# All 32 experts of the first pass in one loop, with an expert of no tokens at each end, and TensorE's three counts in registers

## The reference

```python
logits = h @ w_router + b_router                  # h (320, 1024), 32 experts
top_val, top_idx = lax.top_k(logits, 4)
gates = softmax(top_val)
for e in range(32):                               # what the blocks of rows amount to
    xb = h[tokens of e]
    x_glu, x_lin = jnp.split(xb @ w_gu[e] + b_gu[e], 2, axis=-1)        # 1024 -> 2048
    x_glu, x_lin = jnp.minimum(x_glu, 7.0), jnp.clip(x_lin, -7.0, 7.0)
    act = x_glu * sigmoid(1.702 * x_glu) * (x_lin + 1.0)
    out = (act @ w_down[e] + b_down[e]) * gate                          # 1024 -> 1024
    acc[tokens of e] += out
x = x + gate2 * acc
```

## Time and profile before

| | us |
|---|---|
| median of 3 runs | 1277.75 (1271.48 to 1280.69) |
| the profiled execution | 1283.42 |
| its span in the profile | 1281.6 |
| PE busy | 1108.4 (86%) |
| DVE, ACT, POOL busy | 416.6, 194.3, 44.0 |

### The profile page before, as it was taken

One profiled execution on the slowest core, in us unless ns is written; L12 is line 12 of the kernel. 1 busy time (PEld: TensorE's weight loads), 2 busy tenths in 40 slices (PEclk: granted clock), 3 DMA queues, 4 the chain that ended last, 5 costly groups with the idle time before them and its releaser, 6 DMA issues.

```text
span 1281.6 us, 21966 instructions
## 1 busy us (share of the span) xinstructions
PE 1108.4 (86%) x7288; PEld 463.7 (36%) x7289; DVE 416.6 (33%) x1295; ACT 194.3 (15%) x427; POOL 44.0 (3%) x27
## 2 busy tenths in 40 slices
PE   4999998976858888679979998999999979869986
PEld 0667664643223223223323332333333323223332
DVE  2133635434215222223233224233223323322233
ACT  2323242122101000011101111011111101101100
POOL 0141110002000000000000000000000000000000
PEclk8998997986979989999999999999999999988988
DMA  9963218730979999999999999999999999999992
GB/s 379 344 232 119 91 68 326 280 131 26 395 313 423 422 422 422 422 422 422 421 422 422 421 423 422 421 422 422 422 422 421 422 422 422 422 422 422 421 421 104
DMA packets 76889, 454.99 MB, mean 355 GB/s; under 512 B 9868, under 2 KB 14732, under 8 KB 24524
## 3 DMA queue, kind: packets, MB, share of 16 engines
q1 hardware_dynamic: 70304, 449.76, 85.6%
q10 hardware_dynamic: 6540, 4.60, 1.3%
HBM read 451.17 MB, written 3.17 MB: 355 GB/s over the span
## 4 chain that ended last, share of the span: by engine, by line
PE 58%; DMA 26%; issue 5%; SPq 5%; DVE 4%; ACT 2%; DVEq 0%; POOL 0%; ACTq 0%
DMA ring<-w_gu 20%; PE psum L907 12%; PE psum L941 11%; PE psum L593 6%; PE psum L900 4%; SPq L507 4%; DMA ring<-w_down 4%; PE psum L978 3%; PE psum L862 3%; PE psum L802 3%; PE psum L897 2%; PE psum L602 2%; DMA ring<-w_ada 2%; PE psum L557 2%; PE psum L870 1%
## 5 line engine op out<-in xcount | busy, mean ns | idle before, releaser
L907 PE MATMUL psum<-ring,work 128*32 128x512 f32 (+1 forms) x1792 | 328.8, 632 | 46.2 <-DMA ring<-w_gu 39.1
L941 PE MATMUL psum<-ring,work 128*32 128x256 f32 (+1 forms) x1760 | 205.8, 470 | 22.5 <-issue 11.2
L1699 DVE SCALAR_TENSOR_TENSOR x<-psum,tiny,x 128x256 f32<-128x256 f32 (+1 forms) x512 | 155.2, 376 | 203.0 <-PE psum L978 203.0
L907 PEld LDWEIGHTS psum<-ring,work 128*32 128x32 f32 (+1 forms) x1792 | 84.1, 126 | 247.1 <-issue 141.1
L1668 DVE TENSOR_SCALAR work<-csb 96x128 bf16<-96x128 f32 x64 | 15.4, 280 | 406.3 <-PE psum L907 337.5
L1050 ACT ACTIVATE work<-psum 128x256 f32<-128x256 f32 (+5 forms) x215 | 88.2, 430 | 336.8 <-PE psum L941 210.7
L941 PEld LDWEIGHTS psum<-ring,work 128*32 128x32 f32 (+1 forms) x1760 | 78.3, 123 | 134.6 <-issue 100.1
L1305 ACT ACTIVATE work<-work 128x128 f32<-128x128 f32 (+2 forms) x64 | 24.2, 378 | 574.3 <-DVE work L1683 574.3
L593 PE MATMUL psum<-h,ring 128*128 128x320 f32 x320 | 91.9, 445 | 1.2 <-ACT h L1085 1.2
L978 PE MATMUL psum<-work 32*128 32x320 f32 (+1 forms) x576 | 79.6, 478 | 4.7 <-issue 3.3
L593 PEld LDWEIGHTS psum<-h,ring 128*128 128x128 f32 x320 | 62.3, 196 | 27.4 <-issue 3.7
(11 more groups left out here) (213 smaller groups left out, 704.8 us busy)
## 6 DMA issues: line engine op xcount, KB each, us to landing
ring<-w_gu SPq DMA_DIRECT2D x256, 1024.0 KB, 25.7
ring<-w_down SPq DMA_DIRECT2D x128, 1024.0 KB, 23.4
ring<-w_ada SPq DMA_DIRECT2D x12, 2048.0 KB, 9.0
ring<-w_in SPq DMA_DIRECT2D x7, 2048.0 KB, 30.4
ring<-w_out SPq DMA_DIRECT2D x2, 2048.0 KB, 11.1
x<-xT SPq DMA_DIRECT2D x1, 1280.0 KB, 6.0
yT<-x SPq DMA_DIRECT2D x2, 640.0 KB, 4.1
work<-b_exp ACTq DMA_DIRECT2D x3, 384.0 KB, 16.5
```

Of the source, the lines that this page charges most:

```text
L907: last = mm(o, xg[:, kk, 0:m], cols(ring[:, kk, :]), start=False, stop=kk == KD - 1)
L941: last = mm(o, actT[:, kk, cols], ring[:, GU_UNITS + kk // 2, c1_:c1_ + n], start=False, stop=kk == 7)
L1699: last = stt(x[:, f, cols], bank[SPREAD_BANKS[u]][:, cols], mod[:, 40 + f, sq_:sq_ + 1], x[:, f, cols], ALU.mult, ALU.add)
```

## The change

`passes` runs the first pass as one loop over all 32 experts. What an expert does for its neighbours now happens at both ends too. Ahead of expert 0 stands an expert of no tokens: its output `otok` and its scatter matrix `spread` are zeros that POOL writes, so expert 0's body scatters zeros and DVE adds them to `x`; the semaphores `otok_ready`, `spread_ready` and `acc_ready` start 1, 1 and 8 higher, and the thresholds move with them. Behind expert 31 stands another: `cnti` has a zero ahead of and two behind the 32 counts, `rank` and the constant `stack` have a 33rd column, so expert 31's body gathers and turns an empty selection. PE loads three counts with one instruction (`reg_load`) into registers, once ahead of the loop and then in each expert behind units 0 to 2, for the next expert. Passes 1 and 2 keep their form.

```diff
         def passes(eng, start, expert, finish):
             eng.wait_ge(cnt_ready, 1)
             start(0, 0, 0)
-            expert(0, 0, 0, True, False)
             most = eng.value_load(cmaxi[0:1, 0:1], min_val=0, max_val=T)
-            with eng.Fori(1, NE - 1) as e:
+            with eng.Fori(0, NE) as e:
                 expert(e, e, 0, False, False)
-            expert(NE - 1, NE - 1, 0, False, True)
             finish(NE - 1, 0)
...
             def start(turn, e, b):
+                at = ahead(turn, b)
                 n = count(pe, e)
...
+                by_rows(pe, n, b, lambda groups: (gather(at, groups), turn_x(at, groups)))
+                if isinstance(b, int):
+                    pe.reg_load(counts, cnti[0:1, 0:3])
...
             def expert(turn, e, b, begins, ends):
-                n = count(pe, e)
-                before = None if begins else count(pe, e - 1)
-                after = None if ends else count(pe, e + 1)
-                pe.wait_ge(xg_ready, turn + 1)
-                by_size(pe, n, b, lambda groups: (up_bias(turn, groups), gate_up(0, 3, turn, groups)))
+                if begins:
+                    before, n, after = None, count(pe, e), count(pe, e + 1)
+                else:
+                    before, n, after = [pe.snap(r) for r in counts]
+                at = ahead(turn, b)
+                pe.wait_ge(xg_ready, at + 1)
+                by_size(pe, n, b, lambda groups: (up_bias(at, groups), gate_up(0, 3, turn, groups)))
+                if not ends:
+                    pe.reg_load(counts, cnti[0:1, bass.ds(e + 1, 3)])
                 if not begins:
                     spread_out(0, turn - 1, before, b)
...
             def add(i, turn):
-                if i == 0 and not (isinstance(turn, int) and turn == 0):
-                    v.wait_ge(acc_ready, turn * 8)
+                if i == 0:
+                    v.wait_ge(acc_ready, turn * 8 + 16)
...
-            cp(cnti, bank[5][:, 96:128])
+            nc.vector.memset(rank[:, :, NE:NE + 1], -1.0)
+            nc.vector.memset(cnti[:, 0:1], 0)
+            nc.vector.memset(cnti[:, NE + 1:NE + 3], 0).then_inc(acc_ready, 8)
+            cp(cnti[:, 1:NE + 1], bank[5][:, 96:128])
...
+            g.wait_ge(state_stored, 16 * 2)
+            g.wait_ge(logit_ps, 1)
+            nc.gpsimd.memset(otok[:, 0:256], 0.0).then_inc(otok_ready, 1)
+            nc.gpsimd.memset(spread, 0.0).then_inc(spread_ready, 1)
```

More of the change, by code:

```diff
@@ L440, in count, with ahead @@
         def count(eng, e):
-            return eng.value_load(cnti[0:1, bass.ds(e, 1)], min_val=0, max_val=T)
+            return eng.value_load(cnti[0:1, bass.ds(e + 1, 1)], min_val=0, max_val=T)
+        def ahead(turn, b):
+            return turn if isinstance(b, int) else turn + 1
         def by_size(eng, n, b, body):
@@ L834, in _ @@
             for tt, (t0, n) in enumerate(TILES):
-                last = mm(bank[7][0:n, tt * NE:(tt + 1) * NE], lgT[:, t0:t0 + n], K("stack"), start=True, stop=True)
+                last = mm(bank[7][0:n, tt * NE:(tt + 1) * NE], lgT[:, t0:t0 + n], K("stack")[:, 0:NE], start=True, stop=True)
             last.then_inc(logit_ps, 1)
@@ L989, in scatter @@
                         part(u, FEATURES[4 * i + u], 4, 512, spread_b, False, True).then_inc(sc_ps, 1)
+            counts = [pe.alloc_register(f"count{i}") for i in range(3)]
             def start(turn, e, b):
+                at = ahead(turn, b)
                 n = count(pe, e)
-                pe.wait_ge(pick_ready, turn * 3 + 3)
+                pe.wait_ge(pick_ready, at * 3 + 3)
                 if not isinstance(b, int):
-                    pe.wait_ge(acc_ready, turn * 8)
-                by_rows(pe, n, b, lambda groups: (gather(turn, groups), turn_x(turn, groups)))
+                    pe.wait_ge(acc_ready, turn * 8 + 16)
+                by_rows(pe, n, b, lambda groups: (gather(at, groups), turn_x(at, groups)))
+                if isinstance(b, int):
+                    pe.reg_load(counts, cnti[0:1, 0:3])
             def spread_out(i, turn, n, b):
                 if i == 0:
-                    pe.wait_ge(otok_ready, turn + 1)
-                    pe.wait_ge(spread_ready, turn + 1)
+                    pe.wait_ge(otok_ready, turn + 2)
+                    pe.wait_ge(spread_ready, turn + 2)
                 by_size(pe, n, b, lambda groups: scatter(i, turn, groups))
             def expert(turn, e, b, begins, ends):
-                n = count(pe, e)
-                before = None if begins else count(pe, e - 1)
-                after = None if ends else count(pe, e + 1)
-                pe.wait_ge(xg_ready, turn + 1)
-                by_size(pe, n, b, lambda groups: (up_bias(turn, groups), gate_up(0, 3, turn, groups)))
+                if begins:
[7 more added lines that the diff above has]
+                    pe.reg_load(counts, cnti[0:1, bass.ds(e + 1, 3)])
                 if not begins:
@@ L1024, in expert @@
                 if not ends:
-                    pe.wait_ge(pick_ready, turn * 3 + 6)
-                    by_rows(pe, after, b, lambda groups: gather(turn + 1, groups))
+                    pe.wait_ge(pick_ready, at * 3 + 6)
+                    by_rows(pe, after, b, lambda groups: gather(at + 1, groups))
                 by_size(pe, n, b, lambda groups: (down_bias(turn, groups), turn_act(0, turn, groups), turn_act(1, turn, groups)))
                 if not ends:
-                    by_rows(pe, after, b, lambda groups: turn_x(turn + 1, groups))
+                    by_rows(pe, after, b, lambda groups: turn_x(at + 1, groups))
                 by_size(pe, n, b, lambda groups: down(turn, groups))
@@ L1278, in _, with gathered @@
             part_mid(5)
[L1280 to L1281 removed]
+            def gathered(at, groups):
+                act_.wait_ge(gath_ps, at + 1)
                 if groups == 1:
@@ L1299, in start @@
             def start(turn, e, b):
-                by_rows(act_, count(act_, e), b, lambda groups: (gathered(turn, groups), turned(turn, groups)))
+                by_rows(act_, count(act_, e), b, lambda groups: (gathered(ahead(turn, b), groups), turned(ahead(turn, b), groups)))
             def sigmoids(turn, groups):
@@ L1347, in expert @@
                 if not ends:
-                    by_rows(act_, after, b, lambda groups: gathered(turn + 1, groups))
+                    by_rows(act_, after, b, lambda groups: gathered(ahead(turn, b) + 1, groups))
                 by_size(act_, n, b, lambda groups: activations(turn, groups))
                 if not ends:
-                    by_rows(act_, after, b, lambda groups: turned(turn + 1, groups))
+                    by_rows(act_, after, b, lambda groups: turned(ahead(turn, b) + 1, groups))
                 by_size(act_, n, b, lambda groups: outputs(turn, groups))
@@ L1789, in constants @@
     put("sel", sel.reshape(MLH, MLH * P))
-    put("stack", np.tile(np.eye(NE, dtype=np.float32), (P // NE, 1)))
+    put("stack", np.tile(np.eye(NE, NE + 1, dtype=np.float32), (P // NE, 1)))
     put("iota", np.tile(np.arange(CAP, dtype=np.float32), (P, 1)))
```

32 lines of the change are left out of this document (16 added, 16 removed).

## The result

The changed kernel takes 1703.34 us (median of 4 runs, 1684.14 to 1724.59), the kernel before 1279.16 beside it (1271.48 to 1280.69). The ratio is 1.328, with a 95% interval of 1.315 to 1.342: the change costs a third of the time. The ratio leaves out the slowest of the four, which counts as a slow run, and so compares 1698.97 with 1279.16. The profiled execution has a span of 1682.3 us. The forecast was 1550 with a range to 1690: its side and the mechanism of its likeliest case hold, its size was too small.

The account below looks back on a forecast made before the run. Code refetched in every iteration makes PE bound throughout, hiding the weight transfers (77% busy): 312.3 + 1234 + 11.5 + 1.8 = 1559 us, 1552 on the median, taken as 1550. The 8-in-10 range was 1258 to 1690.

Parts of the forecast that it names:

- likeliest case: PE's loop: a ninth block displaces the loop's code, so every iteration refetches it; 1550 us, own range 1390 to 1700, chance 0.36.
- Term (2): Loop moved to 8 blocks by removing expert 0's copy: every iteration costs like a first pass, 1234 us in place of 958.
- Pieces: Sign in the instruction transfers, 400 to 1200 us: about 8 or 9 an iteration, some 250 in all, if every iteration refetches.
- Waits of 3 us and more inside an expert: Sign in PE's timeline: "issue" waits of this size inside each expert if all refetch, against only one at its bias.
- The share near 0.77: Sign in the DMA share of the loop's stretch: near 0.77 if every iteration refetches, 0.9 with one miss, 1.01 if code stays.
- Only one place is shared: Rival in PE's loop: the ninth block displaces just the first, one miss at each iteration's head; 1354 us, chance 0.25.
- The code stays: Rival: no block of PE's loop is displaced, and the end gains 10.8 us; 1267 us, chance 0.34.
- The start loses: Rival: code stays, but expert 0 has 13.6 us of code waits with transfers idle; 1281 us, chance 0.05.
- (3): Expert 0 on PE's path: scattering zeros and DVE's additions cost about +2 us.
- (4): Behind expert 31: the empty gather, 1.28 us, falls in PE's wait for activations; 1.3 us if that cover were gone.
- (5): Counts at each expert's start: one load cuts "issue" from 1.7 to 1.9 to about 0.6 us, worth 1.1 once at the end.
- (6): Expert 31 run from the loop: 27.8 us in place of 37.5 if the code stays, a gain of 9.7.

Follow-up runs that it names:

- e2: Kernel before with 60 empty waits (30 instructions) at PE's start, so its loop reaches 13 instructions into an eighth block: 1754.45 us, ratio 1.375.
- e3: Changed kernel with 132 empty waits (66 instructions) at PE's start, loop head 7 instructions ahead of a block's start, 8 blocks: 1759.27 us in one execution.
- e1: Changed kernel with 194 empty waits (97 instructions) at PE's start, so the loop touches 7 blocks: 1269.57 us, ratio 0.9943 to the kernel before.
- e4: Changed kernel with 152 empty waits (76 instructions) at PE's start, loop head 3 instructions behind a block's start, 7 blocks: 1269.59 us in one execution.
- e5: e1 with three loads of counts at each expert's head again, and one wait pair more: 1271.56 us, ratio 0.995 to the kernel before.
- e6: Changed kernel with expert 0 written out ahead of the loop again, expert 31 in the loop, 7 blocks without a shift: 1269.82 us, ratio 0.9948.
- e7: Changed kernel shifted by 97 instructions, expert 0 in the loop, expert 31 written out behind it, 7 blocks: 1270.12 us, ratio 0.9945.
- e8: Changed kernel unshifted, 128-row form taken out of PE's branches, loop of 1385 instructions in 7 blocks: 1269.71 us, ratio 0.9966 to the kernel before.
- e9: Changed kernel (8 blocks) with SP's weight transfers for experts 1 to 31 cut to an eighth: 1357.84 us in one execution.
- e10: Changed kernel shifted by 97 instructions (7 blocks), with SP's weight transfers for experts 1 to 31 cut to an eighth: 1140.57 us in one execution.
- e1_again: e1 measured once more beside e5, e6 and e7: 1267.85 us, ratio 0.992 to the kernel before.

## Why the prediction failed in size

**What bounds, and the blocks: right.** The layout counted from six waits (256 instructions a block, starts at 193 + 256 n) says 8 blocks for the changed kernel, e2 and e3, and 7 for e1, e4, e5, e6, e7 and e8. All nine times fall as it says, across an edge of ten instructions. Seven blocks and the one ahead stay; with eight all of the loop and the block ahead are loaded anew, nine pieces in every expert of e3. Whether the store has eight places that a ninth block enters, or seven and a separate one for the block ahead, no run tells.

The Trainium skill ("Runtime: NRT & Kernel Launch", Instruction fetch mechanics) gives 2048 instructions, first in first out, in blocks of 256. The edge between 7 and 8 touched blocks agrees with that. It also calls the cost of crossing into a block mostly hidden; the five waits of rows 3, 13.6 us in one small expert, disagree, and its remark that kernels prefer full unrolling meets a last expert of 37.5 us written out and 27.85 from a loop that stays.

**Term (2), the price of an iteration: the step that failed.** Each iteration was priced as a first pass, which is reached straight on, and the fetch of the loop's head behind the jump back was put at nothing beyond the 1.9 us that a small expert has anyway. The runs show 256.1 us of "issue" at 27 starts there, 9.5 each. The sum was 15 x 37.2 + 13 x 37.5 + 4 x 47 = 1234. Measured are 15 x 37.4 + 13 x 44.0 + 4 x 55.1 = 1354. That the small term holds is luck: nine of the 15 intervals are 41 to 45 us, 43.1 on average, since the head's wait rose from 1.9 to about 10 while those inside fell from 13.6 us to 8.6 (0.88 + 2.44 + 0.61 + 4.63 in the expert from 355.83), and the other six are only 26 to 33 us, around the four starts without a wait. In e3, where no start is spared, a small expert takes 44.6. The medium price was off by 6.5 us, 85 in all. It came from expert 31, whose code is reached straight on and never by a jump back, so it held one miss of 3.54 and no head. In the changed kernel a medium expert from bias to bias, as 1111.94 to 1157.87, has 45.9: a head wait of 9.66 at its end, 1.13 and 3.70 inside, and slow matmuls behind. The large one was off by 8.1, 32 in all: my bounds were 42.1 to 60.9, and I took a value near the low end where the same head wait belonged to it. 85 + 32 + 4 (small) is about the 120 that the experts lack. The profiled execution began them 2.6 us earlier and spent 18.8 us, not 11.5, from the end of the last down to the span's end; it is the fastest of four runs, and the median lies another 19 us higher. Where those 19 us and the 7 at the end come from is open.

The prediction named "up to 31 x 5.96 = 185 us more" for the head, and then left it out of the sum and cut the range at 1690, where 1552 + 185 = 1737 was its own bound. (Between the ends of the waits of rows 3 lie 24.00 / 4 = 6.00 us; 5.96 counts from the expert's start, a small slip.) The L895 group has 257.7 us, of which the sum held 1.9 in each of the 15 small experts, 29 together: 229 more, above that bound. The other open bound, fetches beside less busy transfers being faster, was right in sign by e9. That the waits inside are shorter at a share of 0.77 may be its doing, or that of the long wait at the head, in which blocks can come in ahead; no run separates the two.

Of the 544 us over e10's span, the "issue" waits of L895, L946 and L912 make 393 (256.1 + 91.5 + 51.1, less 5.5 in e10). Most of the rest is PE itself: busy 1199.1 us where e10, with the same matmuls, has 1055.0. Behind a wait of some 10 us PE runs at half the clock for a while, as behind the one that ends at 1157.87:

```profile
1157.80:1162.00 4.20, 4.13 (x12) 1.41 (x14) 0.00 (x0) 0.00 (x0) 0.00 (x0) 0.50 0.02 4
```

The granted clock is 0.50 there, the lower of the two levels (1.2 and 2.4 GHz); over the middle it is 0.83, and 1.00 in e10.

**The signs to look for.** Pieces: "some 250 in all", and there are 264 - 20 = 244 more than in e1: nine an iteration, and four pairs of experts that share nine or less. Waits of 3 us and more inside an expert: one in 18 of the 32, two in five, most often ahead of down, and none in nine, the four large ones and the last among them. The share near 0.77 is 0.77, but partly by luck: 299 of 422 GB/s is 0.71, packets take longer each.

**The rivals.** "Only one place is shared", 1354 us, is out: nine pieces an iteration, not 2. "The code stays" is what e1 runs: 1267 forecast, 1269.57 and 1267.85 measured. "The start loses" is out: expert 0's pass has 24.2 us from its bias to its down, against 21.9 before, and no wait above 1.67; the forecast had 341 for the start of down, e1 shows 336.53. The loop's first pass costs about 5 us when a medium expert makes it (32.9 from bias to bias in e1, against 27.8 in the loop), and expert 1 then takes 17.0 us in place of 37.2. That no hole opens at 341 is a small gain that the forecast called even.

**The small terms.** (3), zeros scattered in expert 0: forecast +2, measured 24.2 - 21.9 = 2.3, of which 0.7 is a longer wait ahead of down (1.67 against 0.98). (4), hidden: the last expert in e1 takes what a medium one in the loop takes. (5), 1.1 us once: three loads leave 1.72 us, e1 none. e5's span is 4.4 above e1_again's (1270.0 against 1265.6), but its experts begin 2.9 us later (312.78 against 309.85), which leaves 1.5. (6), 37.5 to 27.8: 27.85.

## What to carry to other kernels

Count the code of a loop in blocks, from its place and not from its length alone: when a change moves the loop (here by taking 1447 instructions away ahead of it), look at where its head and end fall, and shift it or cut an unused form until the count fits. When a price is taken from a row, ask whether that row was reached in the same way, straight on or by a jump back; and a bound that is named as open belongs in the sum or in the range.

## What the runs showed of the hardware

- PE keeps a loop of 7 blocks of 256 instructions over 29 iterations with no transfer; one of 8 fetches them all and the block ahead, nine pieces, in every iteration of e3 and in most of the changed kernel, also when only two instructions of the eighth are executed (e2). Behind some small experts the head is found and the count is 6 (four times in the changed kernel, nine in e9).
- A jump back onto a block that is gone costs 8 to 11 us beside weight traffic of 299 GB/s, which a large expert shows as two waits (5.42 and 3.99), and 4 to 7 beside 51 GB/s. The whole reload costs 544 us in the one case and 217 in the other.
- A first pass over the loop costs a medium expert about 5 us (no wait above 1.67 in e1), and a small one 18.8 us.
